# Residual steps reordered, low parts moved to GpSimd, and one context norm made earlier in a transformer kernel

## The chip, the cores and the metric

The kernel runs on one core of a Trainium2 chip. Its engines are TensorE (PE in the profile; its weight loads are PEld), VectorE (DVE), ScalarE (ACT), GpSimd (POOL), and SyncE (SP), which only issues loads. The metric is the device time of one execution in microseconds, the median of several runs; lower is better. "At 1961.34" is a point on the profile's axis, counted from the span's start; other times are durations.

## The reference, cut to what matters

The input is 512 tokens of width 1024. Two transformer blocks follow each other; the second one also carries a context of 256 tokens.

```python
def first_block(x, ...):
    for i in range(2):
        x = x + 0.5 * swiglu(rms_norm(x, norm_gains[i, 0]), ...)          # FFN, width 2816
        h = rms_norm(x, norm_gains[i, 1])
        x = x + (stick_breaking_attention(h) if i == 0 else sliding_window_attention(h))
        x = x + 0.5 * swiglu(rms_norm(x, norm_gains[i, 2]), ...)
    return x

def second_block(x, c, ctx, ...):
    for i in range(2):
        shift, scale, gate = ...                      # from c for x, from c_ctx for ctx
        hx = modulate(rms_norm_2(x, norm_g[i]), shift_x, scale_x)
        hc = modulate(rms_norm_2(ctx, norm_g[i]), shift_c, scale_c)
        ox, oc = diff_attention_mixer(hx, hc, ...) if i == 0 else window_gqa_mixer(hx, hc, ...)
        x = x + gate_x * (ox @ w_o[i])
        if i == 0: ctx = ctx + gate_c * (oc @ w_o[i])
    return rms_norm_2(x, final_g)
```

## The kernel before

Activations lie transposed: `x` is 8 tiles of 128 features x 512 tokens, `xc` 8 tiles of 128 x 256 for the context. Every float32 operand of a product is split into a high part and a low part in fp32r, and each product is three matmuls (`three_pass`, L440 to L442: low weight x high input, high x low, high x high). A weight piece (128 x 1024, "half" in the code) is loaded by SP into one of 2 buffers `raw`, ACT copies its high part into one of 4 slots `wh` (`split_hi`, L431), and DVE subtracts to get `wl` (`split_lo`, L435). The wait for a slot is on the product that last used it.

The program is a list of stages made by `make_plan`: setup, FFN 0, stick-breaking attention (`sb`) and its output projection (out), FFN 1, FFN 2, sliding window attention (`sw`) and out, FFN 3, the context's norm and the norm of x, differential attention (diff) and its out (`o0`), two norms, band attention and its out (`o1`), the final norm. Each engine runs its own instruction list in the order in which the code writes it, and semaphores join them. Nothing else sets the order.

What the change touches:

- **out_projection** (L2797 on DVE). Per output tile n of 8: `split_lo` of the piece n + `ahead`, `gained_lo(n-1)` (L2110, the low part of the next stage's input; its high part is `gained_hi`, L1441 on ACT), `add_square(n-1)` (L487, L489, the sum of squares for the next norm), and only then `residual(n)` (L2163, which adds the product in PSUM to x). ACT writes per tile: `split_hi(n + ahead)`, `gained_hi(n)`, `square(n)` (L475). In `o0` each step also has a context half (`who="c"`). PE does 24 triples' worth of k-tiles per output tile, of which the first parts are done inside the attention stage (`out_part`).
- **the next FFN's first piece** (`project(..., norm=m)`) waits for `xlo_done` of each k, that is for `gained_lo(k)`; then follow half of the second piece and the norm's mean (`mean`, L736).
- **final_lo** in the differential and band stages (L2718 and L2720, L2583 on DVE): the low part `act_l` (and `actc_l` for the context) of the attention's output k, from `final_hi` on ACT (L1948, L1949, L1807). PE's `out_part` waits for it through `ready`. In the last head (h = 7) DVE writes these between `combine` (normalises the two softmaxes, L2664 to L2672), `maximum` (L2654, L2657), `p_lo` (L2679) and the split of weights. PE has the stations scores(j), turned(j) (the transposes, L730) and values in between, for query blocks j = 0 to 5.
- **norm** for the context ahead of the differential stage: the mean on PE (L747), Ln and Exp on ACT (L1481, L1484), then per k `scaled` (L2127, DVE), the high part (L1492, ACT), `low` (L2133, DVE). It ends before the norm of x begins, because each engine's list has it first. The stage's first four products are of the context (128 x 256 each, 24 matmuls a piece), the next four of x.

## Time and profile before

| | us |
|---|---|
| median of 3 runs | 2865.72 (2865.26 to 2865.95) |
| the profiled execution | 2864.9 |
| its span | 2863.1 |
| PE busy in the span | 2763.8 (97%) |
| DVE busy | 1627.6 (57%) |
| ACT busy | 1136.9 (40%) |
| POOL busy | 168.6 (6%) |
| granted PE clock, mean of the span | 0.985 of full |

A time between the program's start and its first recorded instruction, 1.8 us here, is in the execution's own time but not in its span. "Busy" of PE counts overlapping matmuls, so 97% says that PE is the engine that the others have to keep fed, and not that it runs at its peak. A sum of savings is made against the profiled execution.

### The profile page before, as it was taken

How to read it: one execution, taken by the hardware profiler on the slowest of the kernel's cores; microseconds unless marked ns; L12 is line 12 of the kernel's file. 1: busy time of each engine (PE TensorE's matmuls, PEld its weight loads, DVE VectorE, ACT ScalarE, POOL GpSimd, SP SyncE). 2: the span in 40 equal slices, each digit the busy share in tenths (PEclk: the TensorE clock that was granted, in tenths of full speed). 3: DMA queues.
4: the chain of work that ended last, by engine and by line, in shares of the span. 5: the costliest groups of instructions: out<-in, count | busy, mean ns of one | idle time of the engine just before them, and what ended most of it. 6: DMA issues, size and time to landing. Idle time of an engine off the chain costs nothing.

```text
span 2863.1 us, 38360 instructions
## 1 busy us (share of the span) xinstructions
PE 2763.8 (97%) x14094; PEld 2284.4 (80%) x14094; DVE 1627.6 (57%) x2504; ACT 1136.9 (40%) x1774; POOL 168.6 (6%) x207
## 2 busy tenths in 40 slices
PE   8999999999999999999998999999999997999998
PEld 7888888887888888888777788887788886778776
DVE  6665466665666454442585544415666666457775
ACT  5232156554222143321464422214455555245443
POOL 0000000000000010000120000000010010010000
PEclk9999999999999999999999999999999998989999
DMA  5444421223444433332211333331111110111112
GB/s 173 139 128 147 129 77 44 60 65 102 133 138 138 146 99 93 97 103 88 70 38 47 89 100 95 96 102 52 52 38 35 46 37 22 52 45 30 45 31 67
DMA packets 329771, 235.27 MB, mean 82 GB/s; under 512 B 8080, under 2 KB 309264, under 8 KB 329552
## 3 DMA queue, kind: packets, MB, share of 16 engines
q1 hardware_dynamic: 321168, 205.50, 24.3%
q0 software_dynamic: 8512, 28.58, 3.5%
q8 instruction: 54, 0.88, 0.1%
q14 instruction: 37, 0.30, 0.0%
HBM read 231.96 MB, written 2.10 MB: 82 GB/s over the span
## 4 chain that ended last, share of the span: by engine, by line
PE 86%; DVE 6%; ACT 5%; issue 2%; POOL 0%; DMA 0%; ACTq 0%; DVEq 0%; SPq 0%; POOLq 0%
PE ps L440 24%; PE ps L442 24%; PE ps L441 24%; PE ps L730 2%; PE ps L1093 2%; PE ps L1240 2%; PE ps L1068 1%; ACT apr L1913 1%; PE ps L840 1%; DVE x L2163 1%; DVE act_l L2110 1%; ACT wh L431 1%; DVE tmp L489 1%; DVE wl L435 1%; PE ps L844 1%
## 5 line engine op out<-in xcount | busy, mean ns | idle before, releaser
L440 PE MATMUL ps<-act_h,wl 128*128 128x512 f32 x2224 | 895.2, 403 | 31.6 <-DVE act_l L2110 16.0
L442 PE MATMUL ps<-act_h,wh 128*128 128x512 f32 x2224 | 870.9, 392 | 0.0
L441 PE MATMUL ps<-act_l,wh 128*128 128x512 f32 x2224 | 870.1, 391 | 0.0
L435 DVE TENSOR_TENSOR wl<-raw,wh 128x1024 fp32r<-128x1024 f32 x382 | 464.1, 1231 | 404.2 <-ACT wh L431 401.2
L431 ACT ACTIVATE wh<-raw 128x1024 fp32r<-128x1024 f32 x382 | 393.4, 1051 | 454.0 <-PE ps L442 364.1
L440 PEld LDWEIGHTS ps<-act_h,wl 128*128 128x128 f32 x2224 | 420.2, 189 | 126.9 <-issue 15.6
L441 PEld LDWEIGHTS ps<-act_l,wh 128*128 128x128 f32 x2224 | 420.5, 189 | 90.1 <-issue 7.9
L442 PEld LDWEIGHTS ps<-act_h,wh 128*128 128x128 f32 x2224 | 419.6, 189 | 89.9
L440 PE MATMUL ps<-h_h,wl 128*128 (+1 forms) x704 | 278.4, 396 | 0.0
L441 PE MATMUL ps<-h_l,wh 128*128 (+1 forms) x704 | 278.4, 396 | 0.0
L442 PE MATMUL ps<-h_h,wh 128*128 (+1 forms) x704 | 278.4, 396 | 0.0
L2180 DVE TENSOR_TENSOR tmp<-ps,tmp 128x512 f32<-128x512 f32 x88 | 60.9, 692 | 319.3 <-PE ps L442 319.3
L1508 ACT ACTIVATE h_h<-tmp 128x512 f32 (+1 forms) x88 | 55.6, 632 | 381.7 <-DVE tmp L2186 381.6
L442 PEld LDWEIGHTS ps<-h_h,wh 128*128 128x128 f32 x704 | 132.3, 188 | 32.3
L441 PEld LDWEIGHTS ps<-h_l,wh 128*128 128x128 f32 x704 | 132.3, 188 | 31.9
L440 PEld LDWEIGHTS ps<-h_h,wl 128*128 128x128 f32 x704 | 132.3, 188 | 31.8
L1503 ACT ACTIVATE tmp<-tmp 128x512 f32<-128x512 f32 x88 | 55.7, 633 | 187.6 <-DVE tmp L2174 187.6
L440 PE MATMUL ps<-actc_h,wl 128*128 128x256 f32 x352 | 107.2, 305 | 4.7 <-DVE actc_l L2133 4.7
L441 PE MATMUL ps<-actc_l,wh 128*128 128x256 f32 x352 | 102.1, 290 | 0.0
L442 PE MATMUL ps<-actc_h,wh 128*128 128x256 f32 x352 | 101.9, 289 | 0.0
L2174 DVE TENSOR_TENSOR tmp<-ps,tmp 128x512 f32<-128x512 f32 x88 | 60.6, 688 | 61.4 <-PE ps L442 49.6
L2191 DVE TENSOR_TENSOR h_l<-tmp,h_h 128x512 fp32r<-128x512 f32 (+1 forms) x88 | 60.6, 688 | 40.4 <-ACT h_h L1508 40.4
(315 smaller groups left out, 3817.2 us busy)
## 6 DMA issues: line engine op xcount, KB each, us to landing
raw<-in_ffn_w_gate_up SPq DMA_DIRECT2D x176, 512.0 KB, 4.0
raw<-in_ffn_w_down SPq DMA_DIRECT2D x88, 512.0 KB, 3.9
raw<-in_a_w_in SPq DMA_DIRECT2D x32, 512.0 KB, 4.0
wmod<-in_w_mod POOLq DMA_DIRECT2D x48, 256.0 KB, 3.4
xc<-in_w_mod POOLq DMA_DIRECT2D x48, 256.0 KB, 3.3
raw<-in_sb_w_in SPq DMA_DIRECT2D x24, 512.0 KB, 4.1
raw<-in_b_w_in SPq DMA_DIRECT2D x20, 512.0 KB, 4.0
raw<-in_w_o SPq DMA_DIRECT2D x16, 512.0 KB, 3.9
```

The lines of the kernel that those rows point to most:

```text
L431: act.activation(wh[:, slot, :], raw[:, slot % RAWS, :], ACT.Copy).then_inc(hi_done[slot], 1)
L435: dve.tensor_tensor(wl[:, slot, :], raw[:, slot % RAWS, :], f32(wh[:, slot, :]), ALU.subtract).then_inc(lo_done[slot], 1)
L440: pe.matmul(bank, w_lo, r_hi, start=start, stop=False, skip_group_check=skip)
L441: pe.matmul(bank, w_hi, r_lo, start=False, stop=False, skip_group_check=skip)
L442: return pe.matmul(bank, w_hi, r_hi, start=False, stop=stop, skip_group_check=skip)
L730: last = pe.transpose(psf[:, bank * SEQ + b * P:bank * SEQ + (b + 1) * P], src(b), fconst(F_IDENT))
L1093: last = pe.matmul(ps[:, 7, c0:c0 + count * P], a_[:, c // 4, tile, v_of(e)], b_[:, e, s_, first * P:(first + count) * P], start=s_ == 0 a ...
L1240: last = pe.matmul(psf[:, KEYS * e + c0:KEYS * e + c1], a_[r, q], b_[r, c0:c1], start=n == 0, stop=n == 2, skip_group_check=True)
L1503: act.activation(tmp[:, u, :], tmp[:, u, :], ACT.Silu).then_inc(sil_done, 1)
L2174: dve.tensor_tensor(tmp[:, u, :], ps[:, 2 * u, :], tmp[:, 5, :], ALU.mult).then_inc(gr_done, 1)
L2180: dve.tensor_tensor(tmp[:, 2 + u, :], ps[:, 2 * u + 1, :], tmp[:, 5, :], ALU.mult).then_inc(ur_done, 1)
L2191: dve.tensor_tensor(h_l[:, i * 2 + u, :], tmp[:, 2 + u, :], f32(h_h[:, i * 2 + u, :]), ALU.subtract).then_inc(hlo_done, 1)
```

## The change

Four things are done.

1. In `out_projection` on DVE, `residual(n)` now comes first in each step, then `gained_lo(n-1)`, `add_square(n-1)` and the split of the piece. Piece 0 is split ahead of the loop, and the last two `add_square` stand behind it.
2. In the last head of the differential stage and the last group of the band stage, `final_lo(0)` to `final_lo(6)` are GpSimd's, written as one block behind its rotary work. DVE keeps `final_lo(7)`, with a wait for the seven others.
3. The context's norm ahead of the differential stage is no stage of its own on any engine. Its mean is a PE matmul right behind FFN 3's own mean, its root (in `root_c`, the second half of `wmod`) an Ln and an Exp on ACT before FFN 3's SiLU, and its eight scaled, high and low parts stand between the weight splits of FFN 3's down projection. For that the down loops of ACT and DVE are written out.
4. The table load before the norm of x is kept where it was.

```diff
@@ build_program @@
+        if st.ctx_norm:
+            st.ctx_norm.early = True
...
+        ssq_c, root_c = wmod[:, 0:CTX], wmod[:, CTX:2 * CTX]
@@ gpsimd, differential(st) @@
+                def final_lo(k):
+                    pool.wait_ge(w.fh, START + 2 * k + 2)
+                    pool.tensor_tensor(act_l[:, k, :], ao[:, k, :], f32(act_h[:, k, :]),
+                                       ALU.subtract).then_inc(w.fl, 1)
+                    pool.tensor_tensor(actc_l[:, k, :], oc[:, k, :], f32(actc_h[:, k, :]),
+                                       ALU.subtract).then_inc(w.fl, 1)
...
                 with pool.Fori(0, 7) as h:
                     head(h, True)
+                for k in range(7):
+                    final_lo(k)
@@ gpsimd, banded(st) @@
+                for k in range(7):
+                    pool.wait_ge(w.fh, base.fh + k + 1)
+                    pool.tensor_tensor(act_l[:, k, :], bw.o[:, k, :], f32(act_h[:, k, :]), ALU.subtract).then_inc(w.fl, 1)
@@ tensor, ffn(st) @@
+                if st.ctx_norm:
+                    pe.wait_ge(cacc_done, START + 8 * st.ctx_norm.before["cres"])
+                    pe.matmul(ps[:, 5, 0:CTX], fconst(F_MEAN1024), ssq_c, start=True, stop=True).then_inc(ms_done, 1)
...
+                if st.ctx_norm:
+                    pe.wait_ge(ln_done, START + st.ctx_norm.n["norm"] + 1)
                 down(0, 0, (0, 1), first=True)
@@ scalar, root(st) and ffn(st) @@
+                if st.following.kind == "ffn" and st.following.ctx_norm:
+                    act.wait_ge(ms_done, START + m + 2)
+                    act.activation(root_c, ps[:, 5, 0:CTX], ACT.Ln, bias=eps_t[:, 0:1]).then_inc(ln_done, 1)
+                    act.wait_ge(ln_done, START + m + 2)
+                    act.activation(root_c, root_c, ACT.Exp, scale=-0.5).then_inc(r_done, 1)
...
+                if st.ctx_norm:
+                    for t in range(4, 20):
+                        split_hi(act, *half(st, 2 * FT + t))
+                        if t > 11:
+                            context_hi(t - 12)
@@ vector, ffn(st) @@
+                elif st.ctx_norm:
+                    for t in range(2, 20):
+                        split_lo(dve, *half(st, 2 * FT + t))
+                        if t > 10:
+                            context_scaled(t - 11)
+                        if t > 11:
+                            context_lo(t - 12)
@@ vector, differential(st) and banded(st) @@
-                        final_lo(0)
...
                 def final_lo(k):
                     dve.wait_ge(w.fh, START + 2 * k + 2)
+                    dve.wait_ge(w.fl, START + 2 * k)
@@ vector, out_projection(st) @@
+                piece(0)
+                for n in range(KT):
+                    residual(st, n, st.banks[n % 4], mod[:, st.layer, 16 + n, 0:1] if st.gated else 1.0, *half(st, n))
+                    if st.ctx:
+                        residual(st, n, st.ctx_banks[n % 4], mod[:, st.layer, 16 + n, 1:2], who="c")
                     if n:
                         if st.tail:
                             gained_lo(st.tail, n - 1)
-                        add_square(dve, st, n - 1)
...
+                        if n < KT - 1:
+                            add_square(dve, st, n - 1)
+                            if st.ctx:
+                                add_square(dve, st, n - 1, "c")
+                        piece(n)
                 if st.tail:
                     gained_lo(st.tail, KT - 1)
-                add_square(dve, st, KT - 1)
-                if st.ctx:
-                    add_square(dve, st, KT - 1, "c")
+                for n in range(KT - 2, KT):
+                    add_square(dve, st, n)
+                    if st.ctx:
+                        add_square(dve, st, n, "c")
```

How this moves instructions is read at three places. The first is DVE at the start of `sw` out, before; `wl` is a split of weights, `hi_done1` is ACT's part of it, `product1` PE's end of tile 1:

```order
L435 TENSOR_TENSOR wl<-raw,wh 128x1024 [waits ctx_in,hi_done0]
L2163 SCALAR_TENSOR_TENSOR x<-ps,x 128x512 [waits product0]
L435 TENSOR_TENSOR wl<-raw,wh 128x1024 [waits hi_done1]
L2110 SCALAR_TENSOR_TENSOR act_l<-x,columns,act_h 128x512 [waits xhi_done]
L487 COPY tmp<-tmp 128x512 [waits sq_done]
L2163 SCALAR_TENSOR_TENSOR x<-ps,x 128x512 [waits product1]
L435 TENSOR_TENSOR wl<-raw,wh 128x1024 [waits hi_done2]
```

and with the change:

```order
L443 TENSOR_TENSOR wl<-raw,wh 128x1024 [waits ctx_in,hi_done0]
L2212 SCALAR_TENSOR_TENSOR x<-ps,x 128x512 [waits product0]
L2212 SCALAR_TENSOR_TENSOR x<-ps,x 128x512 [waits product1]
L2157 SCALAR_TENSOR_TENSOR act_l<-x,columns,act_h 128x512 [waits xhi_done]
L495 COPY tmp<-tmp 128x512 [waits sq_done]
L443 TENSOR_TENSOR wl<-raw,wh 128x1024 [waits hi_done1]
L2212 SCALAR_TENSOR_TENSOR x<-ps,x 128x512 [waits product2]
```

The split that waits for `hi_done1` stood ahead of the residual that waits for `product1`; now it stands three rows behind it.

The second is DVE at the end of FFN 3 (sums of squares in `tmp`), before:

```order
L489 TENSOR_TENSOR tmp<-tmp 128x512 [waits acc_done,sq_done] x2
L2127 SCALAR_TENSOR_TENSOR tmp<-xc,gmod,tmp 128x256 [waits r_done,xlo_done,cacc_done]
L2127 SCALAR_TENSOR_TENSOR tmp<-xc,gmod,tmp 128x256
L2133 SCALAR_TENSOR_TENSOR actc_l<-tmp,mod,actc_h 128x256 [waits xhi_done]
L2127 SCALAR_TENSOR_TENSOR tmp<-xc,gmod,tmp 128x256 [waits xlo_done]
L2133 SCALAR_TENSOR_TENSOR actc_l<-tmp,mod,actc_h 128x256 [waits xhi_done]
```

and with the change (`x` scaled, its low part `act_l`):

```order
L497 TENSOR_TENSOR tmp<-tmp 128x512 [waits acc_done,sq_done] x2
L443 TENSOR_TENSOR wl<-raw,wh 128x1024 [waits hi_done0,xlo_done,cacc_done]
L443 TENSOR_TENSOR wl<-raw,wh 128x1024 [waits hi_done1]
L2176 SCALAR_TENSOR_TENSOR tmp<-x,gmod,tmp 128x512 [waits r_done]
L2176 SCALAR_TENSOR_TENSOR tmp<-x,gmod,tmp 128x512
L2182 SCALAR_TENSOR_TENSOR act_l<-tmp,mod,act_h 128x512 [waits xhi_done]
```

Between the last sum and the split of weights, the sixteen context rows are gone.

The third is DVE in the differential stage's last head, at final_lo(0), before:

```order
L2713 TENSOR_TENSOR oc<-oc,ag 128x256 [waits a_gsc,a_on]
L2714 TENSOR_TENSOR ao<-ao,ag 128x512
L2718 TENSOR_TENSOR act_l<-ao,act_h 128x512 [waits a_fh]
L2720 TENSOR_TENSOR actc_l<-oc,actc_h 128x256
L2664 RECIPROCAL st_nm<-st_den 128x2 [waits a_pe]
L2666 TENSOR_SCALAR st_nm<-st_nm,nlam 128x1 [waits a_rc0]
```

with the change:

```order
L2784 TENSOR_TENSOR oc<-oc,ag 128x256 [waits a_gsc,a_on]
L2785 TENSOR_TENSOR ao<-ao,ag 128x512
L2735 RECIPROCAL st_nm<-st_den 128x2 [waits a_pe]
L2737 TENSOR_SCALAR st_nm<-st_nm,nlam 128x1 [waits a_rc0]
L2740 TENSOR_SCALAR apr<-apr,st_nm 128x768 [waits a_rc1]
L2743 SCALAR_TENSOR_TENSOR apr<-apr,st_nm 128x768 [waits a_pn0]
```

and the block on POOL (its first rows, of 14):

```order
L645 TENSOR_TENSOR act_l<-ao,act_h 128x512 [waits a_fh]
L647 TENSOR_TENSOR actc_l<-oc,actc_h 128x256
L645 TENSOR_TENSOR act_l<-ao,act_h 128x512 [waits a_fh]
L647 TENSOR_TENSOR actc_l<-oc,actc_h 128x256
L645 TENSOR_TENSOR act_l<-ao,act_h 128x512 [waits a_fh]
```

The two subtractions have left DVE's row ahead of the reciprocal that waits for the exponentials (`a_pe`), and wait on POOL for the high parts (`a_fh`) alone.

## Rows read from the trace of the kernel before

**Rows 1.** the waits of PE over the whole run: who waited <- for whom: us, times, longest
```profile
PE ps L440 <- DVE act_l L2110: 16.0, 6, 8.9
...
PE ps L440 <- DVE actc_l L2720: 15.6, 5, 3.9
```

**Rows 2.** timeline of DVE in `sw` out: start, us, what [idle before <- releaser]
```profile
1583.16 0.75 DVE L2110 SCALAR_TENSOR_TENSOR act_l<-x,columns,act_h 128x512 fp32r<-128x512 f32 x1
...
1583.83 0.69 DVE L489 TENSOR_TENSOR tmp<-tmp 128x512 f32<-128x512 f32 x1
...
1584.43 0.69 DVE L2163 SCALAR_TENSOR_TENSOR x<-ps,x 128x512 f32<-128x512 f32 x1
```

**Rows 3.** timeline of ACT in the same step of `sw` out
```profile
1580.94 1.04 ACT L431 ACTIVATE wh<-raw 128x1024 fp32r<-128x1024 f32 x1
...
1585.15 0.72 ACT L1441 ACTIVATE act_h<-x,columns 128x512 fp32r<-128x512 f32 x1 [3.16 <-DVE x L2163]
```

**Rows 4.** timeline of PE, ends of `sb` out and `sw` out
```profile
667.97 0.50 PE L440 MATMUL ps<-act_h,wl 128*128 128x512 f32 x1 [1.78 <-DVE act_l L2110]
...
1603.13 1.02 PE L736 MATMUL ps<-tmp,kf 128*128 128x512 f32 x2
```

**Rows 5.** the waits of PE from 1585 to 1604 alone
```profile
PE ps L440 <- DVE act_l L2110: 4.9, 3, 1.8
```

**Rows 6.** table of windows: busy of PE, PEld, DVE, ACT, POOL; then PEclk, DMA, GB/s
```profile
1595.10:1601.90 6.80, 5.45 (x13) 3.81 (x13) 4.57 (x6) 4.42 (x5) 0.00 (x0) 0.50 0.14 40
...
1850.00:1900.00 50.00, 50.00 (x216) 40.27 (x215) 9.44 (x8) 8.03 (x8) 0.00 (x0) 1.00 0.32 103
...
1967.20:1974.00 6.80, 6.72 (x29) 6.02 (x29) 5.99 (x11) 4.68 (x8) 0.00 (x0) 0.50 0.05 11
...
2390.20:2431.10 40.90, 27.38 (x133) 22.32 (x134) 28.80 (x50) 21.82 (x40) 0.00 (x0) 0.75 0.05 13
```

**Rows 7.** timeline of PE at the differential stage's entry
```profile
1961.34 1.02 PE L747 MATMUL ps<-tmp,kf 128*128 128x512 f32 x2
...
1975.05 0.28 PE L441 MATMUL ps<-actc_l,wh 128*128 128x256 f32 x1
...
1980.97 0.40 PE L440 MATMUL ps<-act_h,wl 128*128 128x512 f32 x1
```

**Rows 8.** timeline of ACT and DVE at that entry
```profile
1959.97 1.28 ACT L1474 ACT_TABLE_LOAD   x1
...
1969.71 1.99 ACT L431 ACTIVATE wh<-raw 128x1024 fp32r<-128x1024 f32 x2
...
1973.16 1.41 DVE L2127 SCALAR_TENSOR_TENSOR tmp<-x,gmod,tmp 128x512 f32<-128x512 f32 x2
...
1983.41 1.63 DVE L2133 SCALAR_TENSOR_TENSOR act_l<-tmp,mod,act_h 128x512 fp32r<-128x512 f32 x2
```

**Rows 9.** timeline of ACT, DVE and PE in the differential stage's last head
```profile
2390.06 0.64 ACT L1948 ACTIVATE act_h<-ao 128x512 fp32r<-128x512 f32 x1
...
2396.59 0.89 ACT L1913 ACTIVATE apr<-ps,st_nm 128x768 f32<-128x768 f32 x1
...
2425.60 0.90 ACT L1913 ACTIVATE apr<-ps,st_nm 128x768 f32<-128x768 f32 x1 [0.40 <-DVE st_nm L2657]
...
2398.78 0.68 DVE L2718 TENSOR_TENSOR act_l<-ao,act_h 128x512 fp32r<-128x512 f32 x1
...
2400.82 1.02 DVE L2672 SCALAR_TENSOR_TENSOR apr<-apr,st_nm 128x768 f32<-128x768 f32 x1
...
2405.08 1.76 DVE L2654 TENSOR_REDUCE st_den<-ps 128x2 f32<-128x1536 f32 x1 [3.24 <-PE ps L1240]
...
2431.07 0.41 PE L730 MATMUL ps<-kf,apr 128*128 128x128 f32 x1
```

**Rows 10.** timeline of POOL and DVE while both work, differential stage's first head
```profile
1993.05 1.28 POOL L625 TENSOR_TENSOR tmp<-tmp 128x512 f32<-128x512 f32 x1 [7.14 <-PE ps L1220]
...
2000.82 1.78 DVE L2689 TENSOR_TENSOR aq_l<-tmp,aq_h 128x512 fp32r<-128x512 f32 x1
```

More of the change, by code:

```diff
@@ L188, in make_plan @@
     plan.stage("end")
+    for st, following in zip(plan.stages, plan.stages[1:] + [None]):
+        st.ctx_norm, st.early = None, False
+        if st.kind == "ffn" and following.kind == "norm" and following.who == "c":
+            st.ctx_norm = following
     for st in plan.stages:
+        if st.ctx_norm:
+            st.ctx_norm.early = True
         if st.kind == "out":
@@ L208, in build_program @@
     last_out = [st for st in plan.stages if st.kind == "out"][-1]
+    early_norm, = [st.n["norm"] for st in stages if st.early]
     def more(st):
@@ L739, in norm @@
             def norm(st):
-                if st.late:
+                if st.late or st.early:
                     return
@@ L1472, in norm @@
                 m = st.n["norm"]
-                if not st.follows_norm:
+                if not st.follows_norm or st.n["norm"] == early_norm + 1:
                     act.preload_act_table_set(LN_EXP)
@@ L2240, in ffn @@
                             modulated(28 + t)
+                elif st.ctx_norm:
[5 more added lines that the diff above has]
+                            context_lo(t - 12)
+                    for t in (20, 21) + ((22, 23) if more(st) else ()):
+                        split_lo(dve, *half(st, 2 * FT + t))
                 else:
@@ L2597, in pair @@
                             q_lo(c + 1)
-                        if j == 2 and c == 7:
-                            final_lo(0)
-                            final_lo(1)
                         if j == 3 and c < 7:
@@ L2608, in pair @@
                             gated(c - 1)
-                        if c == 7 and j > 1:
-                            for k in ((2, 3, 4), (5, 6))[j - 2]:
-                                final_lo(k)
                         if c == 7 and j == 3:
@@ L2737, in head @@
                         gated(h - 1)
-                    if not more:
-                        final_lo(0)
                     combine(h, 2)
@@ L2747, in head @@
                         split_lo(dve, *loop_half(st, 3, g))
-                    else:
-                        final_lo(1)
-                        final_lo(2)
                     combine(h, 3)
@@ L2766, in head @@
                         split_lo(dve, *loop_half(st, 0, h + 2))
-                    if not more:
-                        final_lo(4)
-                        final_lo(5)
                     combine(h, 5)
```

52 lines of the change are left out of this document (37 added, 15 removed).

## The prediction

> **What bounds the kernel now.** I read the page's engine shares first: PE is busy 97% of the span, so an edit on DVE, ACT or POOL pays only where PE waits or where its clock falls. Next the waits of PE: with the load at the start left out (8.9 of the 16.0 us in the first row), some 7 us go to low parts made in the two `out` stages and 15.6 us to the context's low parts in the differential stage's last head [rows 1]. Then the timelines of those places, and last a table of windows for what a wait costs beyond itself: after PE had stood, the granted clock was 0.50 of full (the 1.2 GHz level) for 6.8 us in `sw` out and 6.8 us at the differential entry, and 0.75 over the 40.9 us of the last head, while it was 1.00 in FFN 3 [rows 6]. There 216 matmuls of 512 columns take 50 us, 0.231 each, and DVE and ACT work only 9.4 and 8.0 us of 50. That idle time is what the moved context norm may use.
>
> Each term is the time by which PE comes later or sooner at the end of its place, against the profiled execution (2864.9, 0.8 below the median of 2865.7). They add up, because between these places PE runs back to back.
>
> **1. `out` stages.** Before, ACT and DVE form a ring: the split of a piece's low part waits for ACT's high part, ACT's `gained_hi` waited 3.16 us for the residual [rows 3], and the residual stands behind split, low part (0.75) and sum of squares (0.69) [rows 2]. The ring takes about as long as PE's 24 matmuls (24 x 0.231 = 5.5), so residual(n) never catches up and stays some 11 us behind product(n). With the change the residual depends on the product alone, and behind product 7 stand only residual, high part and low part, 0.69 + 0.72 + 0.75 = 2.2 us [rows 2, 3]. The next FFN asks for k = 7 after 7 x 3 x 0.231 = 4.8 us. The waits go, and nothing else is late next.
> - `sw` out: three waits, 4.9 us [rows 5], and 6.8 us at half clock, which lose 3.4: **-8.3**. The mean at 1603.13 [rows 4] should come that much sooner.
> - `sb` out: 1.78 us [rows 4] and 0.37 just before it (the rest of the 7 us, with the 4.9 and small ones): **-2.15**.
> - `o0`, of the differential stage: add_square(6) now stands between residual(7) and add_square(7), on which the next norm's mean waits. The x half is 0.69 [rows 2], the context's is half the tile, so 0.4: at most +1.1, at least 0 if DVE is ahead by then. ACT's square(7) hides about half: **+0.5**. In `o1` there is no context half and ACT's square hides it: 0.
>
> **2. Entry of the differential stage.** The x mean starts at 1961.34 and the first x product at 1980.97 [rows 7]. Between stand 96 matmuls of 256 columns, which need (1980.97 - 1975.05) / 50 = 0.118 each, 11.3 us at full clock. The other 8.3 us are waits for context low parts and the half clock from 1967.2 to 1974.0 [rows 6]. With the context's norm made long before, PE can start them right behind the mean and reach x at about 1961.3 + 11.3 = 1972.6. Is x ready? DVE's last low part ended at 1985.04, 11.9 after its first scaled x at 1973.16, and that in turn 3.45 behind ACT's split at 1969.71 [rows 8]. With the change that split begins when the table load ends, 1959.97 + 1.28 = 1961.25, so the last low part ends at 1961.25 + 3.45 + 11.9 = 1976.6. PE asks for it at 1972.6 + 4.8 = 1977.4. So it is just ready, with 0.8 us to spare: -8.4. The context's mean now costs a matmul of PE in FFN 3, where PE has no slack, at most +0.5. Its two ACT operations and sixteen each on DVE and ACT sit in the down loop, where these are idle over 80% of the time [rows 6]: 0. The bound from below is 0.8 of slack turned into a wait of up to 2. Term: **-7.9**.
>
> **3. Last head of the differential stage.** final_hi(0) was made at 2390.06, but its low part only at 2398.78, 8.7 us later [rows 9]: it is short (0.68) but stands in DVE's row behind head 6's output and ahead of the reciprocal on which the softmax of this head hangs. PE needs both, and each makes the other late. On POOL, final_lo(0) can begin at 2390.7, and the row of DVE loses a pair (0.68 + 0.42) or two in each step. I walked the four engines' orders by hand with the durations of the trace, POOL's at 1.28 (its one row for this shape in float32 [rows 10]) and half of that for the context. exp(2) stays at 2396.59 (it waits for ACT). From there a step of 768 columns is exp 1.85 (two of 0.9), normalising 2.1 (it ended at 2401.84 and would now end near 2399.7), maximum and scale 1.95, some 5.9 in all, where it took 29.0 / 3 = 9.7 up to exp(5) at 2425.60. With the two table loads of ACT inside the fourth step I get exp(3) at 2402.7, exp(4) at 2410.6, exp(5) at 2417.7 and turned(5) at 2422.2 in place of 2431.07: **-8.9**. Some of that is clock (0.75 over the head). The last wait, for k = 7, stays: DVE makes that one as before. POOL has 7 pairs of 1.9 and about 30 us for them.
>
> The bounds: POOL writing fp32r has no row. As fast as DVE, 0.69, gives another -1; each piece twice as long (2.6) gives +6.9 on this term, three times +16.
>
> What POOL's work does to DVE: in the first head, while POOL worked on SBUF operands, a DVE subtraction of this shape took 1.78 instead of 0.68 [rows 10]. I charged about 1 us for that in all, since DVE's long operations here read PSUM.
>
> The Trainium skill speaks against this edit: "GPSIMD Engine Reference", in its part on elementwise cycle accounting, puts a two-input tensor_tensor on GpSimd at nearly twice VectorE's time and calls it the wrong choice for ordinary elementwise arithmetic. The ratio agrees with the rows (1.28 against 0.68 [rows 9, 10]). By that rule the edit should be left out, and the total would be some 9 us higher; the rows say that the place in the queue costs 8.7 us and the slower engine 0.6.
>
> **4. Band end.** Seven pieces go from 0.69 on DVE to 1.28 on POOL. PE consumes a k of 12 to 16 matmuls in 2.8 to 3.7 us, so POOL keeps up; only k = 3 and 4 are asked for in close succession: **+0.2**, between -0.4 and 7 x 0.59 = +4.1.
>
> **5. Clock.** At the places that get denser PE still stops briefly several times. I allow one new stretch at half clock of 3.4 us, which loses **+1.7**; none to three are possible (0 to +5).
>
> **Sum.** -8.3 - 2.15 + 0.5 - 7.9 - 8.9 + 0.2 + 1.7 = -24.9. The profiled execution comes to 2840.0, the median to 2840.8, so **2841**.
>
> **Rivals.**
> - **GpSimd becomes what PE waits for.** POOL's pieces at 2.6 us, because fp32r output or shared access slows both. For it: DVE's 1.78 [rows 10], so the two do hinder each other. Against it: the 1.28 was measured in just that overlap. The last head loses 6.9, the band 7 x 0.5 = 3.5: 2841 + 10.4 = 2851.4. The Trainium skill, "SBUF — State Buffer", on the two sides of SBUF, has VectorE and GpSimd share a port pair whose lock is held for a whole instruction. The row above agrees in direction; a full block both ways is this case.
> - **More comes back.** No new half clock and POOL near 0.7: 2841 - 1.7 - 1 - 1 = 2837; with the shorter last stretch of the head also at full clock, 2835.
> - **The entry keeps part of its wait.** The 0.8 us of slack are not there: ACT's splits and DVE's scaled parts now start together with the norm's root, and PE, 8 us sooner, stands at k = 1 to 7 for low parts that come every 1.6 us (1.63 for the last [rows 8]) where it asks every 0.7. It waits up to 4 us, and the clock falls for 6.8 us, +3.4. 2841 + 7.4 = 2848.
> - **Slower than before.** Same place as the first, one price: POOL's piece of 512 columns at about 4.8 us (3.8 times its row) and its pair at over 7, above the 5.9 us that a step of the head lasts. Then POOL's block of 7 pairs, 50 us, outlasts the head, PE reaches the products of k = 3 to 6 with none of them ready, and turned(5) and what follows come 27 us later than in my walk; with the band's 7 pieces asked for every 3 us, +12. That is 2841 + 39 = 2880. It decides from pieces of about 4 us (+25).
> - **The moves don't take place:** the order shows that they do.
>
> **Chances.** Forecast 0.66; GpSimd as the bound 0.14; more comes back 0.10; the entry 0.07; slower 0.03. The range that leaves out no more than two in ten takes the forecast with its unknowns (head and clock, -6 to +5), the gain case and most of the entry case: 2834 to 2851. A difference of 0.2% (5.7 us) is about what a measurement of this kernel can tell from none. Only the last case and mishaps that I can't name are not faster by more than that: faster 0.94, same 0.03, slower 0.03.
>
> **What the new profile would show.** `out` stages: no wait of PE for `act_l` at the start of FFN 1 and FFN 3, and the granted clock full there; FFN 3's mean near 1594.8 - 2.15 = 1592.7. Entry: 11.3 us from x mean to the first x product, and scaled x right behind the root. Last head: POOL pieces of 1.3 us, each within 2 us of its high part, and turned(5) some 27 us sooner than 2431 (18.4 from the terms ahead of it, 8.9 here). Wrong is the forecast if POOL's rows there show over 2 us, if PE's waits name POOL, if new waits for x's low parts stand at the entry, or if the granted clock in the head stays at 0.75 or falls further.

## The result, and the profile of the changed kernel

| | before | changed |
|---|---|---|
| median | 2865.49 (2864.68 to 2865.95, 4 runs) | 2842.39 (2838.59 to 2843.59, 4 runs) |
| profiled execution | 2864.9 | 2838.59 |
| its span | 2863.1 | 2836.8 |
| mean granted PE clock | 0.985 | 0.989 |

The ratio is 0.9917, 95% interval 0.9900 to 0.9935. The forecast was 2841, in 2834 to 2851. The executions of the changed kernel spread over 5 us, of which more below.

The waits of PE over the whole run, changed kernel (who waited <- for whom: us, times, longest):

```profile
PE ps L448 <- DVE act_l L2157: 9.1, 1, 9.1
PE ps L750 <- DVE apr L2743: 4.9, 4, 2.6
PE ps L767 <- DVE tmp L497: 4.8, 2, 2.5
PE ps L767 <- DVE wmod L497: 3.1, 1, 3.1
PE ps L448 <- DVE actc_l L2792: 3.1, 1, 3.1
```

Against [rows 1]: the only wait left for `act_l` is the one at the start of the program; of the 15.6 us for the context's low parts, the 3.1 for k = 7 is left. New is the wait of the transposes (L750) for DVE's last operation of normalising (L2743).

To see where the time went I cut the traces at marks that all kernels have (an `x` residual of DVE; the first score of PE in the differential stage, a score being the product of a query and a key) and subtracted the starts. In brackets is the time at the lower clock level (1.2 GHz, "half clock") inside each piece, to 1 us. "Again" and "again2" are two more profiled executions of the changed kernel (the experiments below).

| piece | before | changed | again | again2 |
|---|---|---|---|---|
| start to residual 0 of `sb` out | 633.70 (0) | 633.28 (0) | 633.35 (0) | 632.77 (0) |
| to residual 0 of FFN 1 (`sb` out, FFN 1) | 385.65 (0) | 382.81 (0) | 382.77 (0) | 382.68 (0) |
| to residual 0 of `sw` out (FFN 2, `sw`) | 543.92 (7) | 540.95 (3) | 542.31 (7) | 545.46 (10) |
| to residual 0 of FFN 3 (`sw` out, FFN 3) | 386.85 (7) | 378.89 (0) | 378.90 (0) | 378.90 (0) |
| residual 0 to 7 of FFN 3 | 8.47 (0) | 8.47 (0) | 8.47 (0) | 8.47 (0) |
| to the first score (entry) | 48.74 (7) | 44.04 (7) | 42.78 (3) | 42.79 (3) |
| to residual 0 of `o0` (8 heads) | 443.23 (29) | 437.40 (20) | 439.53 (24) | 439.43 (24) |
| to the end (`o0`, band, `o1`, last norm) | 412.49 (34) | 410.90 (30) | 410.71 (30) | 410.71 (30) |

Two things stand out. The pieces without half clock repeat within 0.2 us, but for the first one, from the start, which varies by 0.6. And the third piece, which no edit touches, varies by 4.5 us within one and the same kernel, along with its time at half clock. These 4.5 us are the net difference between the first profiled execution and the third (2838.59 and 2843.05); among the other pieces, what differs cancels.

In the `out` stages DVE now waits for PE's product. Before residual 7 of `sw` out it is idle for 3.65 us:

```profile
1580.48 0.69 DVE L2212 SCALAR_TENSOR_TENSOR x<-ps,x 128x512 f32<-128x512 f32 x1 [3.65 <-PE ps L450]
```

The mean of FFN 3 starts 31.4 us behind residual 0 of `sw` out, where it took 39.9.

At the entry the timelines of PE, ACT and DVE read:

```profile
1946.89 2.08 PE L767 MATMUL ps<-tmp,kf 128*128 128x512 f32 x2 [2.54 <-DVE tmp L497]
...
1962.05 0.39 PE L448 MATMUL ps<-act_h,wl 128*128 128x512 f32 x1
...
1945.77 1.28 ACT L1506 ACT_TABLE_LOAD   x1
...
1950.53 1.41 DVE L2176 SCALAR_TENSOR_TENSOR tmp<-x,gmod,tmp 128x512 f32<-128x512 f32 x2
...
1960.77 1.62 DVE L2182 SCALAR_TENSOR_TENSOR act_l<-tmp,mod,act_h 128x512 fp32r<-128x512 f32 x2
```

```profile
1946.30:1953.10 6.80, 6.21 (x23) 5.18 (x24) 5.23 (x7) 5.40 (x7) 0.00 (x0) 0.50 0.30 81
```

(The second is a table of windows, columns as in [rows 6].) PE had stood 2.5 us for x's last sum of squares, and did the mean and the first context products at half clock. So x's first product came 15.2 us behind the start of the mean, against 19.6 [rows 7] and against the 11.3 that I forecast. The table load is followed by scaled x 3.5 us after its end, and the last low part ended at 1962.39, long before PE needed it.

In the last head, DVE, POOL and PE in one of its steps:

```profile
2381.25 1.63 POOL L645 TENSOR_TENSOR act_l<-ao,act_h 128x512 fp32r<-128x512 f32 x1 [6.20 <-ACT actc_h L1996]
...
2381.78 1.92 DVE L2743 SCALAR_TENSOR_TENSOR apr<-apr,st_nm 128x768 f32<-128x768 f32 x1
...
2382.84 1.44 POOL L647 TENSOR_TENSOR actc_l<-oc,actc_h 128x256 fp32r<-128x256 f32 x1
...
2384.25 1.28 POOL L645 TENSOR_TENSOR act_l<-ao,act_h 128x512 fp32r<-128x512 f32 x1
...
2405.47 0.88 PE L750 MATMUL ps<-kf,apr 128*128 128x128 f32 x6 [2.63 <-DVE apr L2743]
```

GpSimd's first piece takes 1.63, then DVE's 1.92 where it took 1.02 [rows 9], then GpSimd's context part 1.44. Undisturbed, the three take 1.28, 1.02 and 0.72 (the last is measured in p_wait below), 3.02 us in all, and here they fill the 3.03 us from 2381.25 to 2384.28: the two engines take turns. While DVE then reads PSUM, GpSimd's next piece takes 1.28, the value of [rows 10]. Turned(5) is at 2405.5, 25.6 us sooner than before; I had expected 27.

Turned(5) also parts the row of the 8 heads into a piece that the low parts can change and one behind them (u_pool and p_wait are experiments below; in brackets half clock):

| piece | before | changed | again | again2 | u_pool | p_wait |
|---|---|---|---|---|---|---|
| first score to turned(5) | 423.7 (27) | 417.0 (17) | 417.7 (17) | 417.5 (17) | 425.3 (31) | 415.4 (14) |
| turned(5) to residual 0 of `o0` | 19.5 (2) | 20.4 (3) | 21.9 (7) | 21.9 (7) | 19.5 (3) | 20.3 (3) |

### The profile page after: what moved, and what is told of

Read it like the earlier page. It is cut to its first block, busy times and chain, and to the rows that moved or that the text cites. A ratio compares the mean times of both kernels' runs of the same rounds, so it can differ in the third digit from the quotient of the medians.

```text
span 2836.8 us, 38321 instructions
## 1 busy us (share of the span) xinstructions
PE 2751.6 (97%) x14094; PEld 2276.1 (80%) x14094; DVE 1623.9 (57%) x2483; ACT 1136.0 (40%) x1774; POOL 196.2 (7%) x228
## 4 chain that ended last, share of the span: by engine, by line
PE 89%; DVE 5%; ACT 4%; issue 1%; DMA 0%; POOL 0%; ACTq 0%; DVEq 0%; SPq 0%; POOLq 0%
PE ps L448 25%; PE ps L449 25%; PE ps L450 25%; PE ps L750 2%; PE ps L1118 2%; PE ps L1265 2%; PE ps L1093 1%; ACT apr L1960 1%; PE ps L865 1%; PE ps L869 1%; DVE tmp L497 1%; PE ps L1245 1%; DVE wl L443 1%; PE ps L1099 1%; DVE act_l L2157 1%
## 5 line engine op out<-in xcount | busy, mean ns | idle before, releaser
L448 PEld LDWEIGHTS ps<-act_h,wl 128*128 128x128 f32 x2224 | 419.6, 189 | 106.8 <-issue 11.3
L2223 DVE TENSOR_TENSOR tmp<-ps,tmp 128x512 f32<-128x512 f32 x88 | 60.6, 688 | 61.1 <-PE ps L450 48.5
```

Of the source, the lines that this page charges most:

```text
L448: pe.matmul(bank, w_lo, r_hi, start=start, stop=False, skip_group_check=skip)
L2223: dve.tensor_tensor(tmp[:, u, :], ps[:, 2 * u, :], tmp[:, 5, :], ALU.mult).then_inc(gr_done, 1)
```

## The experiments

All times beside a kernel are medians of 4 or 5 executions, with the lowest and the highest; a piece is from the one profiled execution of each kernel. The kernel before had medians of 2864.97, 2865.07 and 2864.92 in the three groups. A stretch "first score to residual 0" is the row of the 8 heads in the table above.

### The changed kernel again

> The changed kernel itself, once more, so that the others stand beside it on one chip. Its first profiled execution was 2838.6, the others 2842.1 to 2843.6. Theory: the 3 to 4 us between them are half-clock stretches that come and go (one of 3.4 us beside PE at work costs 1.7), at places that the edit doesn't touch, as in the sliding window attention, where before had two and the changed kernel one. Then a second trace has the same waits of PE within 0.3 us and another list of stretches at 0.50. Rival: a wait of PE differs, by 3 us at one place. Median expected 2842, in 2839 to 2844.

> The changed kernel once more, on the chip of the three beside it. The earlier medians are 2842.4 (4 runs) and 2840.0 (5 runs). If what moves them is half-clock stretches that depend on where the program stands when a wait comes, this one lies in 2839.5 to 2843 again, and the trace shows the same waits of PE within 0.3 us but another sum of half-clock stretches (62.9 and 66.0 so far). Rival: chips differ, then before on this chip has moved with it.

Medians 2840.02 (2837.78 to 2842.09) and 2843.05 (2839.16 to 2843.36). The waits of PE are the same ones, with two exceptions: the 4.9 us for L2743 are 7.0 in both, and in the sliding window attention again2 has one of 1.9 us that is under 0.5 in the other two:

```profile
PE ps L980 <- DVE sw_pr L2522: 1.9, 1, 1.9
```

Windows of 60 us in the sliding window attention, of changed, again and p_wait (below):

```profile
1495.00:1555.00 60.00, 53.53 (x362) 45.67 (x362) 37.70 (x70) 27.42 (x73) 2.60 (x2) 0.97 0.12 36
```

```profile
1495.00:1555.00 60.00, 53.61 (x357) 46.04 (x356) 37.59 (x70) 27.31 (x72) 2.58 (x2) 0.94 0.13 36
```

```profile
1495.00:1555.00 60.00, 53.16 (x350) 45.80 (x349) 37.29 (x70) 27.32 (x72) 2.58 (x2) 0.91 0.12 36
```

The same stretch of the program at a mean clock of 0.97, 0.94 and 0.91. Over the span the time at half clock was 61.1, 64.2 and 67.6 us in the three traces of the changed kernel, 83.6 before. Where the third piece grows can be read from DVE's starts: from changed to again in one step of 1.4 us (near 1540), from changed to again2 in three steps of 1.5 us (near 1413, 1527 and 1540). The first and the last of the three lie at stretches of half clock that changed has not; the middle one is the wait for `sw_pr`. So the expectation that all waits agree within 0.3 us did not hold, and whether that wait follows from the clock ahead of it is not shown. The rival that chips differ is out: before did not move. Consequence: single edits are judged by their piece of the trace, and a median difference under 3 us between two of these kernels decides nothing.

### Only the order of the out stages undone

```diff
                 for n in range(KT):
+                    piece(n)
+                    if n: gained_lo, add_square of n - 1
                     residual(st, n, ...)
-                    if n: gained_lo, add_square of n - 1, piece(n)
...
```

> Only the order of the out stages goes back: split, low part, sum of squares, then the residual; the rest is as changed. By the comparison of the two traces the new order is worth 3.1 (sb out), 8.4 (sw out, 3.4 of it clock) and costs 0.5 (o0): 11.0 slower than the changed kernel, 2853.4. By the forecast's own terms 10.0. Rival: the residual ring wasn't the cause and the sw gain came with the moved context norm or by luck of the clock: under 5 slower. PE's waits for act_l at the start of FFN 1 and FFN 3 return with 2 and 3 to 4 entries by the first theory, not by the rival.

2851.52 (2850.56 to 2853.4), ratio 0.9953 (0.9940 to 0.9967) to before, so 11.5 slower than "again" on the same chip. By pieces: `sb` out and FFN 1 385.51 (+2.7), `sw` out and FFN 3 387.19 with 7 us at half clock (+8.3), the entry 41.22 without half clock, the last row 412.68 (+2.0; see the edit of tile 6 below). The waits are back:

```profile
PE ps L448 <- DVE act_l L2157: 15.7, 6, 8.9
```

And DVE's residuals of `sw` out come at the pace of the ring again, one in 5.35 us, with no wait for PE's product:

```profile
1583.35 0.68 DVE L2212 SCALAR_TENSOR_TENSOR x<-ps,x 128x512 f32<-128x512 f32 x1
...
1588.70 0.68 DVE L2212 SCALAR_TENSOR_TENSOR x<-ps,x 128x512 f32<-128x512 f32 x1
```

The order in front of the residual was the cause, through the ring. The rival, that the gain came with the moved norm or by luck of the clock, is out.

### Only the context's norm undone

```diff
-        if st.ctx_norm:
-            st.ctx_norm.early = True
+        st.ctx_norm = None
...
```

> Only the context's norm goes back ahead of the differential stage. The comparison of the traces gives its move 4.7 (the forecast had 7.9, since it took the 96 matmuls of the context at full clock and PE had 6.8 us at half clock there in both kernels): 4.7 slower than the changed kernel, 2847. Rival, the forecast's number: 7.9 slower, 2850.3, if the half clock at the entry was chance in the one trace. It is also expected that the PE matmul in FFN 3 is given back, 0.2 to 0.5.

2850.09 (2846.37 to 2851.95): 10.1 slower than "again" by the medians. Its profiled execution was its fastest, 2846.4, and there the entry is 49.19 against 42.79, so +6.4, and FFN 3 378.44 against 378.90: the one extra matmul costs the 0.5 that I had put at the most. Between x's mean and first x product:

```profile
1948.57:1968.17 19.60, 17.69 (x99) 14.86 (x98) 16.89 (x29) 11.80 (x20) 0.00 (x0) 0.77 0.20 55
```

(clock 0.77). In the kernel with the head undone, where the clock happened not to fall, the same stretch is

```profile
1947.56:1959.88 12.32, 12.32 (x98) 11.84 (x99) 10.30 (x14) 8.02 (x11) 0.00 (x0) 1.00 0.31 86
```

and in the changed kernel again

```profile
1948.29:1962.20 13.91, 13.91 (x98) 13.01 (x99) 12.21 (x17) 8.38 (x12) 0.00 (x0) 0.88 0.27 77
```

12.3 us is 1.0 more than the forecast's 11.3, which left out what the mean itself takes. Against before, whose entry had 6.8 us of half clock, the entry is shorter by 7.9 where the clock did not fall, and by 6.0 or 4.7 with 3.4 or 6.8 us of half clock. Undone alone the move gives 6.4, between the 4.7 and the 7.9 of the expectation. Why the medians differ by as much as 10.1 is open beyond their spread.

### Only the low parts of the last differential head undone

```diff
-                for k in range(7):
-                    final_lo(k)          # on GpSimd
+                    final_lo(0) ... final_lo(6) in DVE's last head, as before
```

> Only the low parts of the differential stage's last head go back to DVE, the band's stay on GpSimd. The traces give 7.3 for this edit (forecast 8.9): 2849.7. Rival: since DVE's last operation of normalising took 1.9 in place of 1.02 beside GpSimd five times, the edit is worth hardly anything by itself and the shift came from the clock: under 4 slower, below 2846. PE's waits for actc_l return with about 12 to 15 us in four or five entries by the first.

2846.09 (2845.1 to 2850.69), 6.1 slower than "again". First score to residual 0: 444.77 with 34 us at half clock, against 439.5: the edit gives 5.3, neither 7.3 nor under 4. Up to turned(5) it gives 7.7, and 2.4 of them are lost behind it, where "again" has 7 us at half clock and this kernel 3. The waits are back:

```profile
PE ps L448 <- DVE actc_l L2789: 15.5, 5, 3.9
```

### GpSimd beside DVE's PSUM operations

```diff
                 for k in range(7):
+                    pool.wait_ge(w.pn, START + 7 * 6 + (1, 2, 2, 3, 4, 4, 5)[k] + 1)
                     final_lo(k)
```

> GpSimd's low parts in the last differential head wait, besides the high part, for the end of DVE's normalising (k = 0 for that of query block 1, k = 1 and 2 for 2, k = 3 for 3, k = 4 and 5 for 4, k = 6 for 5), so that they run beside DVE's maximum, which reads PSUM, and not beside its last operation of normalising (three SBUF operands), which took 1.9 in place of 1.02. Theory, the two engines keep each other out when both work on SBUF: that operation is back at 1.02 in all steps, GpSimd's context parts at 0.72, and the first score of head 0 to turned(5) shrinks from 417.0 to 417.7 to about 415: 2.5 faster than the changed kernel, 2837.5. Rival: the lower pieces now come 1 to 2 us later and PE waits for those (2.5 us more in actc_l waits): same or 1 slower, 2840 to 2841.

DVE and POOL in the step that was shown above:

```profile
2382.85 1.02 DVE L2744 SCALAR_TENSOR_TENSOR apr<-apr,st_nm 128x768 f32<-128x768 f32 x1
2383.78 1.75 DVE L2726 TENSOR_REDUCE st_den<-ps 128x2 f32<-128x1536 f32 x1
...
2383.94 1.27 POOL L645 TENSOR_TENSOR act_l<-ao,act_h 128x512 fp32r<-128x512 f32 x1 [7.30 <-DVE apr L2744]
2385.17 0.72 POOL L647 TENSOR_TENSOR actc_l<-oc,actc_h 128x256 fp32r<-128x256 f32 x1
...
2385.95 0.50 PE L448 MATMUL ps<-act_h,wl 128*128 128x512 f32 x1 [1.15 <-POOL actc_l L647]
```

The four wide DVE operations are at 1.02 (1.90 to 1.93 in "again"), the narrow one at 0.49 (1.58), all seven context parts at 0.72 to 0.74. The 8 heads shrink from 439.5 to 435.8, with 17 in place of 24 us at half clock. Of these 3.7 us, 2.2 lie ahead of turned(5), which was expected at about 415 and came at 415.4. The other 1.5 lie behind it, where the edit does nothing and "again" has 3.4 us more at half clock; the first trace of the changed kernel has not, and against that one the edit gives 1.6 in all. PE waits 3.2 us for GpSimd in four places, and the wait for L2744 falls from 7.0 to 2.5. The median is 2839.09 (2835.85 to 2840.1): only 0.9 below "again", and its profiled execution had 10 us at half clock in the untouched piece with the attention, where "again" had 7 (543.8 against 542.3 us). The mechanism is shown by the rows, its size, 1.6 to 2.2 us, by the pieces of the trace; the median alone would not have told.

### GpSimd's piece twice as long

```diff
+                    pool.wait_ge(w.fl, START + 2 * k)
+                    pool.tensor_tensor(act_l[:, 7, :], ao[:, k, :], f32(act_h[:, k, :]), ALU.subtract)
                     pool.tensor_tensor(act_l[:, k, :], ao[:, k, :], f32(act_h[:, k, :]), ...)
```

> GpSimd makes each x low part of the last differential head twice (once into a place that is overwritten later), so a pair takes 3.2 us in place of 1.9 to 2.0. It prices the forecast's rival that GpSimd is what PE waits for. By the walk with which the forecast was made, 1.3 more a pair gives 3 to 4 us (6.9 at 1.9 more): 2843 to 2844. Rival: GpSimd has the slack of a whole step (7 us a step in the trace), nothing waits, under 1 us.

The 8 heads take 439.50, as in the changed kernel (439.53): nothing, though PE now waits 6.0 us for GpSimd (one wait of 0.9 in the changed kernel). The median is 2843.97, but its trace is already 3.0 us late when FFN 3 ends, so that is the clock upstream. My walk was wrong here: DVE's L2745 was held up less in two of the five steps (1.38 and 1.36), and what PE waited more for GpSimd it waited less for DVE.

### Tile 6's sums of squares ahead of residual 7 in `o0`

```diff
+                    if n == KT - 1 and st.ctx:
+                        add_square(dve, st, n - 1)
+                        add_square(dve, st, n - 1, "c")
                     residual(st, n, st.banks[n % 4], ...)
...
```

> In the out stage of the differential layer alone, the sums of squares of tile 6 go back ahead of residual 7. The traces have 0.54 more from the last residual to the context's mean than before. Theory: 0.5 faster, which the median can't show (2839.5), but the wait of PE for the context's sum falls from 3.1 to 2.6, where before had 2.57. Rival: residual 7 comes later by the same 0.7 and nothing is gained.

2842.85 (2841.83 to 2845.51). The wait of PE is 2.56 and was 3.11 in "again", as expected:

```profile
2479.91 0.70 PE L767 MATMUL ps<-wmod,kf 128*128 128x256 f32 x2 [2.56 <-DVE wmod L497]
```

```profile
2480.27 0.70 PE L767 MATMUL ps<-wmod,kf 128*128 128x256 f32 x2 [3.11 <-DVE wmod L497]
```

But from the context's residual 7 of `o0` to residual 0 of `o1` the trace has 316.81 with it and 314.82 without:

```profile
2478.05:2794.86 316.81, 297.85 (x1906) 245.06 (x1907) 223.81 (x403) 153.93 (x330) 39.61 (x30) 0.96 0.13 37
```

```profile
2477.87:2792.69 314.82, 296.43 (x1906) 243.03 (x1907) 224.50 (x405) 153.98 (x330) 39.59 (x30) 0.97 0.14 38
```

The same work at 0.96 and 0.97 of the clock (24 and 20 us at half), 2.0 us apart. The three changed kernels with the sums of squares in this place have 316.76, 316.81 and 316.86 there, seven without it 314.77 to 314.96. (Before has the same order and 315.34, with the band's low parts on DVE, of which below.) So the order that I had charged with 0.5 is the better one here.

Where the 2.0 us arise can be read from DVE's starts: 0.5 are gained at the mean, then 1.2 are lost where the band stage's first scores begin and 1.3 in its last group. In both places the kernel with the edit is at half clock throughout and the other one in part. Here are both places, first "again", then with the edit:

```profile
2539.20:2546.00 6.80, 4.91 (x23) 3.14 (x24) 4.12 (x11) 3.09 (x9) 0.98 (x1) 0.75 0.00 0
2750.80:2761.00 10.20, 10.20 (x61) 9.11 (x59) 5.25 (x13) 3.01 (x8) 0.00 (x0) 0.67 0.38 104
```

```profile
2539.40:2546.20 6.80, 5.48 (x22) 3.81 (x22) 3.36 (x8) 2.34 (x7) 0.36 (x1) 0.50 0.00 0
2751.00:2761.20 10.20, 9.88 (x48) 9.06 (x48) 4.63 (x11) 3.13 (x10) 0.00 (x0) 0.50 0.37 104
```

The first of the two losses is not the edit's alone: two kernels without it (the next one, and the one with the last head undone) have it too, 1.3 us at the same place, and stand at 316.18 and 316.23. What decides which of the two courses the clock takes is not shown.

### The first context product ahead of x's mean

```diff
@@ tensor, norm(st) of x @@
+                if st.next_kind == "diff":
+                    (waits for bank 0, the piece and the context's low parts)
+                    the 24 matmuls of context piece 0, then_inc(A.pc, 1)
@@ tensor, differential(st) @@
-                for t in range(4):
+                for t in range(1, 4):
                     part(0, t, t, "c").then_inc(w.pc, 1)
```

> At the differential stage's entry PE does the first context product (24 matmuls of 256 columns, 2.8 us) before x's mean and not behind it, in the 2.5 us for which it waited for the last sum of squares. Theory: the wait of 2.5 goes, and with it the half clock behind it (6.8 us in one trace of the changed kernel, 3.4 in the other, none in two of the kernels with a part undone), worth 0 to 3.4; x's low parts, one in 1.45 us, are then the next thing late, up to 1.5: 2 to 4 faster, 2837. Rival: x's mean comes 0.3 later, so x's parts do too, and PE waits for these what it saved: within 1 us, 2840.

2838.50 (2837.42 to 2839.51), and from the last residual of FFN 3 to the first score 39.78 in place of 42.8:

```profile
1946.62 1.02 PE L776 MATMUL ps<-tmp,kf 128*128 128x512 f32 x2
...
1959.73 0.50 PE L448 MATMUL ps<-act_h,wl 128*128 128x512 f32 x1 [0.15 <-DVE act_l L2191]
...
1961.18 0.50 PE L448 MATMUL ps<-act_h,wl 128*128 128x512 f32 x1 [0.47 <-DVE act_l L2191]
```

The mean has no wait before it, no half clock follows (1.00 in the window 1943.80 to 1956.01), and x's low parts are late by 0.6 in all. The three kernels with this edit have no half clock behind the mean; of the nine others with the moved norm two have none there. The entry gains 3.0 us, but in this trace the stretch behind the context's residual 7 is 1.4 us longer than in "again" (316.18, see above), and `o0` up to there 1.0 longer. The profiled execution, 2838.35, is little below the first one of the changed kernel (2838.59): it has 4.3 us less at the entry, but 2.1 more in the 8 heads and 2.3 more in the last piece.

### Both together, and all three

> The changed kernel with both edits that shortened their stretch of the trace: GpSimd's low parts wait for DVE's normalising (first score of the differential stage to the first residual of its out stage 435.8 in place of 439.5 us), and the first context product ahead of x's mean (last residual of FFN 3 to the first score 39.8 in place of 42.8). Theory, terms at different places add up: 6.7 faster by the trace, and at least 4 by the median: 2834 to 2836. Rival: the parts showed only 0.9 and 1.5 in the medians, since what is saved comes back as half clock elsewhere: 2837.5 to 2838.5.

> As the one before, with the sums of squares of tile 6 ahead of residual 7 in the differential layer's out stage. The trace gave this edit 0.5 at the context's mean and then a half-clock stretch of 3.4 us more in the band stage. Theory: 0.5 faster than the one before, which the medians can't tell: within 1 of it. Rival: a mean reached 0.5 sooner makes the clock fall longer, 1 to 2 slower than the one before, as the single edit was 2.8 slower than the changed kernel.

Two edits: 2835.14 (2834.05 to 2836.12), ratio 0.9896 (0.9881 to 0.9911), 7.9 faster than the changed kernel on the same chip, and the fastest here. That is what the theory of adding up had (2834 to 2836), and not its rival (2837.5 to 2838.5). Entry 39.79, the 8 heads 435.71, each as in its single kernel, 53.7 us at half clock in the span. Its waits in these places:

```profile
PE ps L751 <- DVE apr L2753: 3.3, 3, 1.7
PE ps L448 <- POOL actc_l L647: 3.3, 4, 1.2
```

All three: 2838.43 (2836.93 to 2839.81), 3.3 slower again, more than either expectation had. By the traces 2.0 of that is the stretch behind `o0`, as with the single edit of tile 6, and 1.4 is the untouched third piece.

### Only the band's low parts undone

```diff
-                for k in range(7): act_l of the band stage on GpSimd
+                    final_lo(0) ... final_lo(6) in DVE's last group, as before
```

> Only the band stage's seven low parts go back to DVE. The traces of before and of the changed kernel show the same shift at the first and the last residual of the last out stage, within 0.1 us (forecast +0.2). Theory: no difference from the changed kernel beyond the noise, within 1.5 us, and the stretch from the band stage's start to the end equal within 0.5 but for the clock. Rival: on GpSimd they save PE a wait of 0.35 and 0.40 at the transposes of the last group: 0.7 slower than the changed kernel with them back on DVE.

2840.62 (2838.42 to 2841.38), 2.4 faster than the changed kernel on this chip, and 313.74 against 314.80 us from the context's residual 7 of `o0` to residual 0 of `o1`, each with 20 us at half clock. So GpSimd costs 1.1 us in the band stage, the other sign than the rival's and outside the theory's 0.5; most of the rest of the 2.4 is the untouched third piece (543.90 against 545.46). In the changed kernel (again2) PE waits for it, and for DVE beside it:

```profile
2777.99 0.74 PE L750 MATMUL ps<-kf,bw_pr 128*128 128x128 f32 x5 [0.86 <-DVE bw_pt_l L2642]
...
2782.35 0.50 PE L448 MATMUL ps<-act_h,wl 128*128 128x512 f32 x1 [0.55 <-POOL act_l L699]
```

Beside GpSimd's pieces DVE's operations on SBUF are held up here as well, down to one of 2 columns. The first two rows are of again2, the third is the same DVE operation in this kernel:

```profile
2773.03 3.79 POOL L699 TENSOR_TENSOR act_l<-bw_o,act_h 128x512 fp32r<-128x512 f32 x3 [41.09 <-ACT act_h L1854]
...
2774.37 1.21 DVE L2620 SCALAR_TENSOR_TENSOR bw_nm<-bw_mx,nsinks 128x2 f32<-128x2 f32 x1
```

```profile
2773.65 0.16 DVE L2617 SCALAR_TENSOR_TENSOR bw_nm<-bw_mx,nsinks 128x2 f32<-128x2 f32 x1
```

The next one, of 2 columns too, took 1.22 in place of 0.16, and two weight splits 4.51 in place of 2.36.

The two faster edits with the band's low parts on DVE were not run together.

## Why the prediction was right, and which of its steps were not

The total was right (24.9 forecast against the profiled execution, 26.3 measured, 24.2 and 21.9 in the other two traces), and so was the case: the four edits do what they say, GpSimd doesn't become the bound. That the total is so near is partly luck. Against the first trace the entry and the last head gave 3.7 and 3.1 us less than forecast. The `out` stages, `o0` with the band, and the start gave 3.6 more, and the rest is an untouched piece that came out 3.0 shorter where 1.7 had been added for the clock. By term:

| term | forecast | before to changed, three traces | undone alone |
|---|---|---|---|
| `sb` out | -2.15 | -2.8, -2.9, -3.0 | 2.7 |
| `sw` out, and the extra mean in FFN 3 | -8.3 and +0.5 | -8.0 in all three | 8.3 |
| entry | -8.4 | -4.7, -6.0, -5.9 | 6.4 |
| last head | -8.9 | -5.8, -3.7, -3.8 | 5.3 |
| `o0` end, band, `o1` | +0.7 | -1.6, -1.8, -1.8 | order 2.0, band -1.1 |
| clock, beyond these | +1.7 | -3.0, -1.6, +1.5 in the untouched piece | |
| start, to residual 0 of `sb` out | 0 | -0.4, -0.4, -0.9 | |

- **`out` stages: right**, by the mechanism and nearly by the size. (PE has 24 matmuls per output tile, 8 triples, and not the 24 triples named in the description of the kernel: residuals 5 to 7 of `sb` out, which wait for PE in the changed kernel, come 5.6 us apart.) `sb` out was 0.7 short: I took the idle time that stands in brackets, 1.78 and 0.37. The starts give more. The matmul at 667.97 came 2.2 us behind the one ahead of it in place of 0.23, so a wait costs its bracket and, with the matmul behind it, some 0.2 to 0.3 more. Over the two waits that is most of the missing part.
- **Entry: the mechanism right, the size 2.4 to 3.7 short, most of it by the clock.** From x's mean to the first x product stand 12.3 us where the clock did not fall, not 11.3: I had left out the mean's own time. The whole entry was then 7.9 shorter than before, against 8.4. I had removed the half clock of 1967 to 1974 [rows 6] together with the context's waits. But PE already stands 2.5 us for x's last sum just there, which no part of the change touches, and in the three traces the clock falls behind it (3.4 to 6.8 us). The general +1.7 was the only thing set aside for it. That scaled x begins 3.5 us behind the table load, and that its last low part ends 11.9 behind that, held to 0.1 us: no wait of PE for them exists (the 1.63 that the rival read as one low part is two), and the rival "the entry keeps part of its wait" named the wrong cause for a number (2848) that did not come.
- **Last head: the mis-sized term**, 3 to 5 us too much at residual 0 of `o0`. Up to turned(5), where the walk ended, 8.9 were forecast and 6.7, 6.1 and 6.2 measured; the other 0.9 to 2.4 us were lost behind it, at half clock. The walk had one cost wrong: "about 1 us in all" for what GpSimd's work does to DVE. I argued that DVE's long operations there read PSUM. The last one of normalising doesn't: it reads and writes SBUF, stands on the path from the exponentials to PE's transposes, and starts when GpSimd is at work on a high part that ACT has just released. It lost 0.9 four times and 1.1 once. With GpSimd waiting for it, turned(5) was 8.3 sooner than before, counted from the first score, within 0.6 of the walk. [Rows 10] had shown the size of it, 1.78 for 0.68, and I charged less than that once for all five steps. Those rows I also misread for GpSimd's side: the DVE operation beside the 1.28 at 1993.05 reads PSUM (`tmp<-ps,tmp`), so that row was no overlap of the kind. The one that was is this, and it kept its time too while DVE lost 1.1:

```profile
2000.76 1.29 POOL L628 TENSOR_TENSOR tmp<-tmp 128x512 f32<-128x512 f32 x1
```

- **GpSimd as the bound: rightly unlikely, wrongly priced.** Its pieces took 1.27 to 1.63, the context's 0.72 to 1.44, so the 1.28 of the float32 row held for fp32r. But 1.3 us more a pair cost nothing measurable where the walk gave 3 to 4. Of the prediction's signs of being wrong, "if PE's waits name POOL" came true, with one wait of 0.9 us and no loss to show for it; no piece took over 2 us, and the granted clock in the head rose from 0.75 to 0.85. The case on the slower side began at pieces of about 4 us, and none was seen.
- **`o0` end: right as a wait** (3.11 against 2.57), **wrong as a time**, by 2.5: the new order gained 2.0 where 0.5 was charged, through half clock in two places of the band stage. **Band:** +1.1 for +0.2, inside its bounds, with the same hindrance as in the last head (0.16 becomes 1.21).
- **The range** was right to reach to both sides: the untouched piece alone moves by 4.5 us from execution to execution.

The Trainium skill, "SBUF — State Buffer", on the two sides of SBUF, has the rule that the shared port pair is held for a whole instruction and the other engine blocks fully. The rows of the last head agree: 1.02 becomes 1.9 and 0.72 becomes 1.44, and both go back when the two no longer meet. In the forecast I had tied that rule to GpSimd being late; it was DVE that it delayed. The Trainium skill, "GPSIMD Engine Reference", on elementwise cycle accounting, advises against elementwise work on GpSimd. By the runs that is right for the band stage (+1.1) and not for the last head, where DVE's queue was what PE waited for: 7.7 us gained up to turned(5) and 9.9 with the two engines kept apart, 5.3 and 9.0 with what the clock did behind it.

## What to carry to other kernels

A short operation on the path can gain on an engine whose queue is empty, even a slower one, where the first engine's queue is what the path waits for; where it isn't, as in the band stage, it costs. Look at which operation of the first engine it meets in SBUF, and let it start behind that one. Put first in a queue what depends on the bound engine alone, and last what only a later norm wants. Where the bound engine must wait for a sum, give it a product that needs nothing from it. And where the clock makes one kernel differ from itself by 4.5 us, compare pieces of the traces with their time at half clock, not totals.

## What the runs showed of the hardware

- In these rows a GpSimd subtraction and a DVE operation with all its operands in SBUF take turns: a DVE operation of 768 columns took 1.90 to 1.93 in place of 1.02, one of 2 columns 1.21 in place of 0.16, a GpSimd one of 256 columns 1.44 in place of 0.72. The duration in the profile thus holds the time for which an operation is kept out. Beside a maximum that reads PSUM (1.75) both kept their time (1.27 and 0.72).
- The time at half clock is not a fixed property of a kernel. One and the same kernel had 3, 7 and 10 us of it in the same stretch, which took 540.9, 542.3 and 545.5 us; over the span it had 61.1 to 67.6. An edit that moves a wait by 0.5 us made the stretch behind it 2.0 us longer, in three kernels.
- Half clock need not cost time: the kernel with the first context product moved had 25 us of it up to turned(5), and the changed kernel again 17, and both took 417.4 to 417.7 us.
